# A two-layer diffusion backbone on one core: first projection with features outermost, modulation by feature halves, down matrices in 8 KB rows

## What is computed

```
m = silu(cond) @ w_mod + b_mod            # w_mod (1024, 6 * 1024) per layer, split in 6:
                                          # shift, scale, gate of attention, then of the experts
h = x * (1 + scale) + shift
z = h @ w_in_ab                           # layer 0: 1024 -> 1184 (latents, q, k, v)
x = LayerNorm(alpha * x + gate * attention(z))
hid = silu(h @ w_gate[e]) * (h @ w_up[e]) # 16 experts, 1024 -> 512, two of them for each token
y   = (hid * gates) @ w_down[e]           # 512 -> 1024
x = LayerNorm(alpha * x + gate * y)
```

## Time and profile before

| | us |
|---|---|
| three executions | 791.24, 795.42, 796.65 |
| their median | 795.42 |
| the profiled execution | 793.16 |
| its span, first to last instruction | 791.4 |

### The profile page before, as it was taken

The page is one execution under the profiler, slowest core; times in us unless marked ns, Lnnn a source line. Parts: engine busy times, 40 slices in busy tenths (PEclk is TensorE's granted clock), DMA queues, the critical chain, the costliest instruction groups (busy, mean ns, idle before and its releaser), DMA issues.

```text
span 791.4 us, 9516 instructions
## 1 busy us (share of the span) xinstructions
PE 734.0 (93%) x3745; PEld 345.0 (44%) x3745; DVE 237.2 (30%) x551; ACT 157.5 (20%) x408; POOL 73.1 (9%) x126
## 2 busy tenths in 40 slices
PE   4699899897999999998799999998999999998896
PEld 1345444455444443443234554454544434442432
DVE  0003544455310010100436228484501001000255
ACT  0201321325011110120103132343211101110201
POOL 0000000000200001102200110000200002101020
PEclk9899899997999999999999999999899999999998
DMA  8999999915499999999999999963299999999993
GB/s 324 397 322 410 410 409 419 417 77 213 186 420 416 417 422 415 421 416 416 419 399 379 409 410 418 397 239 144 98 420 416 422 418 416 422 416 419 415 409 116
DMA packets 67906, 287.40 MB, mean 363 GB/s; under 512 B 6636, under 2 KB 12268, under 8 KB 51988
## 3 DMA queue, kind: packets, MB, share of 16 engines
q1 hardware_dynamic: 63828, 275.54, 86.6%
q10 hardware_dynamic: 2880, 7.03, 2.2%
q0 software_dynamic: 1152, 4.19, 1.3%
HBM read 278.93 MB, written 7.82 MB: 362 GB/s over the span
## 4 chain that ended last, share of the span: by engine, by line
PE 51%; SPq 31%; DMA 9%; DVE 5%; ACT 2%; issue 2%; POOL 0%; DVEq 0%; ACTq 0%
PE bank L1171 14%; SPq L638 12%; PE bank L1207 7%; PE bank L987 7%; SPq L633 6%; DMA ring<-in_exp_w_up 6%; PE bank L838 5%; SPq L634 4%; PE bank L1138 4%; DMA ring<-in_w_mod 3%; PE bank L725 3%; SPq L598 3%; SPq L602 2%; PE bank L966 1%; PE bank L943 1%
## 5 line engine op out<-in xcount | busy, mean ns | idle before, releaser
L1171 PE MATMUL bank<-ring,arena 128*64 128x512 f32 x1024 | 226.2, 597 | 7.8 <-DMA ring<-in_exp_w_up 7.8
L1171 PEld LDWEIGHTS bank<-ring,arena 128*64 128x64 f32 x1024 | 73.5, 138 | 156.5 <-issue 151.5
L1207 PE MATMUL bank<-ring,arena 128*64 128x512 f32 x512 | 113.8, 595 | 6.8 <-DMA ring<-in_exp_w_down 5.7
L1787 DVE TENSOR_TENSOR arena<-bank,arena 128x256 f32<-128x256 f32 x32 | 13.6, 425 | 218.8 <-ACT arena L1993 218.5
L1207 PEld LDWEIGHTS bank<-ring,arena 128*64 128x64 f32 x512 | 36.3, 137 | 73.9 <-issue 66.0
L1138 PE MATMUL bank<-arena 128*128 128x128 f32 x512 | 63.5, 279 | 0.0
L1138 PEld LDWEIGHTS bank<-arena 128*128 128x128 f32 x512 | 61.1, 196 | 1.2 <-issue 0.7
L725 PE MATMUL bank<-ring,cwin 128*32 128x512 f32 x384 | 50.4, 665 | 11.0 <-DMA ring<-in_w_mod 10.4
L1884 ACT ACTIVATE arena<-bank 128x512 f32<-128x512 f32 (+5 forms) x65 | 34.8, 559 | 116.2 <-PE bank L838 32.6
L1993 ACT ACTIVATE arena<-bank 128x256 f32<-128x256 f32 x32 | 12.3, 383 | 219.2 <-PE bank L1171 219.2
L1803 DVE COPY arena<-bank 128x512 f32<-128x512 f32 x14 | 9.7, 691 | 121.9 <-PE bank L1207 121.9
(11 more groups left out here) (200 smaller groups left out, 652.7 us busy)
## 6 DMA issues: line engine op xcount, KB each, us to landing
ring<-in_exp_w_gate SPq DMA_DIRECT2D x62, 1024.0 KB, 20.6
ring<-in_exp_w_up SPq DMA_DIRECT2D x62, 1024.0 KB, 20.3
ring<-in_exp_w_down SPq DMA_DIRECT2D x60, 1024.0 KB, 22.5
ring<-in_w_mod SPq DMA_DIRECT2D x24, 2048.0 KB, 21.5
expert_rows<-arena ACTq DMA_DIRECT2D x12, 512.0 KB, 7.8
ring<-in_w_out_ab SPq DMA_DIRECT2D x2, 2048.0 KB, 23.6
ring<-in_exp_w_down SPq DMA_DIRECT2D x8, 512.0 KB, 15.0
ring<-in_w_in_c SPq DMA_DIRECT2D x2, 2048.0 KB, 18.0
```

The costliest lines, as they stand in the source:

```text
L1171: mm = nc.tensor.matmul(pb(key)[SLOTS * hf:SLOTS * (hf + 1), :], xeT[b][:, k * P + SLOTS * a:k * P + SLOTS * (a + 1)], w[:, :, k % 4, hf * ...
L1207: mm = nc.tensor.matmul(pb(key)[SLOTS * a:SLOTS * (a + 1), :], hp[:, c:c + SLOTS], w[:, a, kf % 2, hf * HALF:(hf + 1) * HALF], start=(kf = ...
```

## The change

1. **Modulation ahead of the first projection by feature halves.** The four blocks of `w_mod` become `top` blocks: all 1024 input features by 512 columns, read in rows of 2 KB. `top_chunks(0)` takes those for output features 0 to 511 of shift and scale, `top_chunks(1)` the others. The columns `ab`, the turning of `x` and the modulated `hT` follow by halves (`top_ab`, `even_rows_turned`, `modulated_columns` with q).
2. **First projection with features outermost.** `w_in_ab` is loaded in three blocks by features (3, 3 and 2 of the 8 tiles of 128), whole rows of 1184 columns, 4.7 KB. `project_even` sums into six banks at once. Part 0 needs only the first feature half and stands between the two halves of the modulation. The last part has its feature loop innermost, so the banks finish one after the other.
3. **Down matrices in rows of 8 KB.** Partition p now holds hidden features 4p to 4p + 3, so two of them are one run of 8 KB. So that the turned hidden layer matches, `gate_up` reads its moving operand with `r` outside `m`: every fourth column (16 bytes apart) instead of 256 adjacent ones. Its products stay 64 by 512 and their number is the same.

The diff, cut to its core:

```diff
-    order = [("mod", 0, c) for c in MOD_PIECES[0]] + [("win", 0, b) for b in range(3)]
+    order = [("top", 0, 0), ("top", 0, 2), ("win", 0, 0), ("top", 0, 1), ("top", 0, 3), ("win", 0, 1), ("win", 0, 2)]
...
+WIN_K = (0, 3, 6, 8)
...
-        w_down = i_["exp_w_down"].rearrange("l e (k p) c -> (l e) p k c", p=P)
+        w_down = i_["exp_w_down"].rearrange("l e (p k) c -> (l e) p k c", p=P)
...
+                if kind == "top":
+                    sp.dma_start(dst.rearrange("p (k c) -> p k c", k=KD),
+                                 w_mod[l, :, :, b * HALF:(b + 1) * HALF]).then_inc(got(n)[0], 16)
+                elif (kind, l) == ("win", 0):
+                    k0, k1 = WIN_K[b:b + 2]
+                    sp.dma_start(dst[:, 0:(k1 - k0) * AB_IN].rearrange("p (k c) -> p k c", c=AB_IN),
+                                 w_in[0][:, k0:k1, :]).then_inc(got(n)[0], 16)
...
-                if n == 3:
+                if n == 1:
                     for g, name in enumerate(("x_prompt", "x_sample")):
...
+            def top_chunks(h, used=None):
...
+                for c in (h, 2 + h):
+                    n = index[("top", 0, c)]
+                    pe.wait_ge(*got(n))
+                    w = block_ap(n).rearrange("p (k c) -> p k c", k=KD)
+                    for k in range(KD):
+                        j = k % 4
+                        mm = nc.tensor.matmul(out[32 * j:32 * j + 32, :], cwin[:, k, 24 - 2 * c:56 - 2 * c], w[:, k, :],
+                                              start=(c == h and k < 4), stop=False, skip_group_check=True)
...
+            def project_even(part):
...
+                if part < 2:
+                    for k in range(k0, k1):
+                        for g in range(G):
+                            for b in range(len(WIN[0])):
+                                step(k, b, g)
+                else:
+                    for b in range(len(WIN[0])):
+                        for g in range(G):
+                            for k in range(k0, k1):
+                                step(k, b, g)
...
-                    w = block_ap(n + k // 4).rearrange("p (w k f) -> p w k f", w=2, k=4)
+                    w = block_ap(n + k // 4).rearrange("p (w k m r) -> p w k r m", w=2, k=4, r=4)
...
-                                              w[:, :, k % 4, hf * 256:(hf + 1) * 256],
+                                              w[:, :, k % 4, 2 * hf:2 * hf + 2, :],
...
-                    modulation(0, 0)
-                    pe.wait_ge(*saved(("mod", 0, 0)))
-                    mod_columns(0, 0)
-                modulated(l, 0)
-                if l == 0:
-                    project(0)
+                    top_chunks(0)
+                    even_rows_turned(0)
+                    project_even(0)
+                    top_chunks(1, index[("win", 0, 0)])
+                    even_rows_turned(1)
+                    project_even(1)
+                    project_even(2)
                     modulation(0, 1, (index[("win", 0, len(WIN[0]) - 1)],))
```

More of the change, by code:

```diff
@@ L211, in plan_turns @@
     t = Turns()
-    t.use(("mod", 0, 0), 7)
     t.use(("lnT",), 5)
-    t.use(("modT", 0, 0), 6)
+    for h in range(2):
+        t.use(("top", h), 7)
+        t.use(("topT", h), 6)
+        for g in range(G):
+            t.use(("hT", 0, 0, g, h), 6 + g if h else 2 * g)
     for l in range(DEPTH):
         for s in range(2):
-            for g in range(G):
-                for q in range(2):
-                    t.use(("hT", l, s, g, q), 2 * g + q)
+            if (l, s) != (0, 0):
+                for g in range(G):
+                    for q in range(2):
+                        t.use(("hT", l, s, g, q), 2 * g + q)
             if s == 0:
@@ L748, in modulation @@
                                  start=False, stop=True, skip_group_check=True).then_inc(*fill(key))
+            def top_chunks(h, used=None):
+                key = ("top", h)
+                room(pe, key)
+                out = pb(key)
+                for c in (h, 2 + h):
[6 more added lines that the diff above has]
+                                              start=(c == h and k < 4), stop=False, skip_group_check=True)
+                        if (c, k) == (h, 0) and used is not None:
+                            mm.then_inc(*release(used))
+                    mm.then_inc(*release(n))
+                bias = tri[0:DEPTH * N_MOD, 0:1].to_broadcast([DEPTH * N_MOD, 32]) if h else \
+                    cst(C_BIAS, 32, DEPTH * N_MOD)
+                nc.tensor.matmul(out[0:32, :], bias, rows[0:DEPTH * N_MOD, :],
+                                 start=False, stop=True, skip_group_check=True).then_inc(*fill(key))
+                pe.wait_ge(*saved(key))
+                turn_rows(("topT", h), mods[0], C_SEL, 8)
             def turn_rows(key, src, c0, n):
@@ L824, in project_odd, with even_rows_turned @@
+            def even_rows_turned(h):
+                pe.wait_ge(s_x, 32)
+                for g in range(G):
+                    rows_turned(0, 0, g, h)
             def project_odd():
@@ L1387, in _, with top_ab @@
             V = nc.vector
+            def top_ab(h):
+                key = ("topT", h)
+                shift, scale = (mod_cols(key)[:, a, :, h] for a in range(2))
+                a_, b_ = (ab[:, 0, a].rearrange("p g (h q) -> p g h q", h=2)[:, :, h] for a in range(2))
+                dve.wait_ge(*full(key))
+                V.tensor_scalar(a_, scale, 1.0, None, ALU.add)
+                V.tensor_copy(b_, shift).then_inc(*drain(key))
+                dve.wait_ge(*saved(key))
+                dve.sem_inc(s_ab2 if h else s_ab, 1)
             def mod_ab(l, s):
@@ L1409, in mod_ab, with modulated_columns @@
+                ch.then(V.tensor_scalar(sc, scale, 1.0, None, ALU.add))
+                for g in range(G):
+                    V.tensor_tensor(a_[:, g], sc[:, g], lnT[:, t - 1, 0], ALU.mult)
+                    last = V.tensor_tensor(b_[:, g], sc[:, g], lnT[:, t - 1, 1], ALU.mult)
+                ch.then(last)
+                V.tensor_tensor(b_, b_, shift, ALU.add).then_inc(*drain(key))
+                dve.wait_ge(*saved(key))
                 dve.sem_inc(s_ab, 1)
-            def modulated_columns(l, s):
+            def modulated_columns(l, s, q=1):
```

96 lines of the change are left out of this document (44 added, 52 removed).

## The result

| | before | changed |
|---|---|---|
| median of the executions, us | 795.33 | 1016.26 |
| lowest to highest, us | 791.24 to 796.65 | 1015.74 to 1018.1 |
| ratio, 95% interval | | 1.279 (1.274 to 1.284) |
| span of the profiled execution, us | 791.4 | 1014.5 |

What follows compares the result with a forecast made beforehand. Transfers were taken to set the pace outside the attention stages. The start (-1.2 us) and down rows (-3.4) gave -4.6 on the profiled 793.16, 788.6, hence a median of 791 us, range 784 to 802.

Steps and rivals of the forecast that it cites:

- step 4: Read of every fourth column in `gate_up`: cost between nothing and twice the time (+13.7 us a pair); taken as nothing.
- the slow side: Strided read in `gate_up` slow: 0.16 for a doubling (985 us), 0.05 for something between (1.15 gives 798, 1.35 gives 842).
- The rival's own sum: Doubled `gate_up` time: 109.8 - 14.6 = 95.2 us a layer, 190 in all, less 1.2 at the start: 985 us; chance 0.16.
- the slack: Experts: PE time hidden behind transfers, put at 14.6 us in layer 0 and 14.5 in layer 1.
- eight pairs at PE's own pace: Experts of layer 0: from 202.62 us they would end at 401.9, against last down products at 416.50.
- step 1: Projection and modulation by halves at the start: projection earlier but hidden by transfers, worth 0 on the path.
- two of my signs: Start: chain through a `w_mod` transfer ending within 2 us of 98; new PE waits for `w_mod` before 90 us.
- three us earlier: End of the first projection: 65.5 us instead of 68.8, with PE beginning near 26 instead of 36.8.
- step 2: Loads at the start, same bytes in other rows: +1.3, -1.0 and -1.5 us, together -1.2 us.
- the two terms of +1.3 and -1.0: Start loads: `w_mod` in 2 KB rows costs +1.3 us; `w_in_ab` in 4.7 KB rows gains 1.0 us.
- The -1.5 us for the hole: Slow DMA stretch at 40 to 48 us around the small loads: partly closed, -1.5 us, between 0 and -4.3.
- step 3: Down matrices in 8 KB rows: expert transfers at 422 instead of 418 GB/s, -1.7 us a layer, -3.4 for two.

Runs made afterwards that it cites:

- steps: A kernel of products alone, with moving operands at various steps; float32 on the whole array took 904 ns a row at step 4, 433 with adjacent columns.
- front_only: The changed kernel with 4 KB down rows and adjacent gate and up reads put back; 794.52 us, ratio 1.0005 to the kernel before.
- front_warm: `front_only` with nine products that nobody uses put into PE's waits at the start; 796.01 us, ratio 1.0013 to the kernel before.
- rows_only: The kernel before with only the down matrix loads changed, to runs of 8 KB; 792.68 us, ratio 0.9981.

## Why the prediction was wrong

**The strided read (step 4).** This is the step that failed, and all the loss is in it. I bounded the cost at nothing and at a factor of two, and took nothing. The measured factor is 2.10. The reason for taking nothing was "PE can take at least twice the data that `gate_up` asks for": four strips read 512 columns each in the time of two. The `steps` kernel shows what is wrong with this. The strips' reads are independent, so four at once say nothing of how fast one of them can be. Each strip with adjacent columns is bound by its columns, and no row of the trace had a strip bound by its read. There was no evidence for a reserve within one stream, and the chance of 0.21 for the slow side was far too small. The statement of "Advanced Engine Details and Errata" (SBUF cachelines) in the Trainium skill, at least two hits on a 16-byte line needed to absorb the access latency, pointed at the mechanism. For float32 the trace agrees: two a piece cost 1.05, one costs 2.09. For bfloat16 it does not: two a piece cost 2.1, and it takes four (1.06). The free reach of 4 float32, which I had set against it from the Trainium skill, did not hold: that step costs 2.09.

**The rival's own sum** gave 985 us for a doubling, and 1016 were measured. Two terms were off. The factor is 2.10 and not 2: 0.10 x 13.73 x 16 = 22 us. And the slack was 8.2 us a layer, not 14.6: eight pairs at 39.98 us are 319.8, the layer took 326.2, so 6.4 us of other products (gates and spreading) stand in the last pairs, 5.5 us in layer 1, and my "eight pairs at PE's own pace" left them out. In the kernel before, PE's own work from the first gate product to the last down product was therefore 199.3 + 6.4 = 205.7 of 213.9 us. With 6.4 and 5.5 us less slack, 12 us, the sum is 985 + 22 + 12 = 1019, within 3 us of the measurement. That (28.80 - 13.73) x 8 - 8.2 gives the 112.3 us of layer 0 is no further proof, since the 8.2 comes from the same rows. A check from other rows stood on the page of the kernel before all along:

```profile
L1171 PE MATMUL bank<-ring,arena 128*64 128x512 f32 x1024 | 226.2, 597 | 7.8 <-DMA ring<-in_exp_w_up 7.8
L1207 PE MATMUL bank<-ring,arena 128*64 128x512 f32 x512 | 113.8, 595 | 6.8 <-DMA ring<-in_exp_w_down 5.7
```

The waits of gate, up and down products add up to 14.6 us for both layers, near 7 for each, and not 14.6 for one.

**The earlier projection (step 1).** "On the path worth 0" came out: 1.0005 in `front_only`, 1.0013 in `front_warm`. Only `front_warm` gets there by the mechanism that I named, an earlier projection hidden by the transfers. In the change and in `front_only` there was no earlier projection to hide, and two of my signs did not appear (a chain through a `w_mod` transfer near 98 us, new waits for `w_mod` before 90 us), so the 0 there is in part luck. PE began at 25.94, as said, but part 0 took 14.68 us and not 12.0 (36 of the 96 rows that took 32.05), and the rest 21.4 and not 20.0. The stretches of the changed kernel's trace (granted clock third from the end, then DMA share and GB/s):

```profile
24.00:32.00 8.00, 6.99 (x16) 3.76 (x15) 1.37 (x4) 1.50 (x4) 0.00 (x0) 0.57 1.05 387
32.00:36.00 4.00, 4.00 (x13) 2.28 (x12) 0.00 (x0) 0.00 (x0) 0.00 (x0) 1.00 1.06 410
40.00:48.00 8.00, 6.72 (x50) 2.76 (x49) 0.93 (x3) 0.00 (x0) 0.00 (x0) 1.00 0.72 198
48.00:100.00 52.00, 48.39 (x267) 24.24 (x268) 19.66 (x61) 11.85 (x41) 1.62 (x2) 0.90 1.03 410
```

From 24 to 32 us the granted clock is 0.57 of 2.4 GHz on average, most of it at the lower level of 1.2 GHz. What PE did before was wait: for the blocks, for the copy, for the columns. From 48 to 52 us, after the waits of the second half, it is 0.52 and 0.63 (by 2 us). With products in these waits the granted clock is 1.00 from 8 to 76 us, and the projection ends at 64.0. The kernel before has such a stretch too, 0.50 to 0.76 from 32 to 36 us, but its projection begins behind it, at 36.76, and has the full clock from 38 us on. The change moved the projection into it, and the term "three us earlier" became 1.3 us later. I read 32 rows at 84.62 in 5.35 us as a wait for the transfer. The profile shows no such wait there; it shows the clock, 0.50 from 84.6 to 87.0 us and 0.89 from there to 90.

**The same bytes in other rows (step 2).** Up to 40 us the changed kernel moves 12.9 MB from 8 us on, the kernel before 12.8. So the two terms of +1.3 and -1.0 nearly cancel, as said. From 10 to 16 us, while the first `w_mod` blocks come in, it is 391 against 413 GB/s; on 8.4 MB that would be 1.1 us, near the +1.3. The -1.5 us for the hole is refuted: 198 against 189 GB/s. SP came to the small loads at 28.0 instead of 30.1 us, but each then waited for room, and the next large load was issued at 44.7, not earlier.

**8 KB rows (step 3).** Predicted 422 GB/s and -1.7 us a layer; measured 421 and, from the first gate product to the last block of gate and up, 191.2 to 189.8 and 191.1 to 189.7: -1.4 us for each layer. Right in mechanism and near in size; the median of `rows_only` moved by 1.6 us, at the limit of the measurement. In the changed kernel nothing of it is left, since DMA no longer sets the pace.

## What to carry to other kernels

A change of layout that helps transfers has to be paid by whoever reads the data. Look at the innermost step of every matmul operand before anything else, and of each 16 bytes that it touches let it use at least two float32, or four bfloat16 (two bfloat16 ran at half rate). Here, reading the two needed neighbours together instead of one column of each group at a time was worth some 222 us. Where the trace of before has no row of a new kind of access, a reserve inferred from parallel streams is none: measure the access by itself. Starting work sooner in a stage that a queue of transfers paces buys only waits (`front_warm`). And before rows of two traces are compared, or a long row is called a wait, look at the granted clock of that stretch.

## What the runs showed of the hardware

- A MATMUL row takes the longer of two times: its columns' (433 ns for 512 in float32, 219 in bfloat16, at the full clock) and about 1.8 ns for each 16-byte piece of SBUF that the moving operand touches. Steps of 8 and 16 elements, where each piece holds one column, are only 2% dearer than that (921 against 904 ns, 926 against 909).
- The price of a piece did not follow TensorE's clock: rows of 512 pieces took 904 ns at 2.4 GHz and 909 at 1.2 (L62 and L102 of `steps`).
- Column strips pay separately: the factor for a step of 4 float32 is 2.09, 2.08 and 2.06 for one, two and four strips.
- HBM to SBUF ran at 384 GB/s with rows of 2 KB, 410 with 4 KB and 422 with 8 KB; with gate, up and down all in rows of 8 KB, 421 (`rows_only`).
- The eleven small loads at the start cost some 3 us of transfer time also when spread over three places: 4.3 us in one lump (8 us at 189 instead of 410 GB/s), less the 1.2 us that spreading them gave back.
